# Output projections of both mixers as three passes on split operands, their residual rows through DRAM, and two narrow projections in two passes

## What is computed

```python
def gdn_mixer(x, w_in, conv_w, a_log, dt_bias, norm_w, w_out):
    p = x @ w_in                                  # [T, 6160]; its last 16 columns are b_logit and a_logit
    qkv = causal_conv_silu(p[..., :GDN_QKV], conv_w)
    ...
    o = gated_delta_rule(q, k, v, g, beta)        # chunked scan over the tokens
    o = gated_rmsnorm(o, norm_w, gate)
    return o.reshape(B, T, GDN_VAL).astype(x.dtype) @ w_out     # [T,2048] @ [2048,1024]

def gla_mixer(x, w_in, w_gk_up, b_gk, norm_w, w_out):
    p = x @ w_in                                  # its last 16 columns are gk_low
    gk_logit = (gk_low @ w_gk_up).astype(f32) + b_gk.astype(f32)
    ...
    return o.reshape(B, T, GLA_VAL).astype(x.dtype) @ w_out     # [T,1024] @ [1024,1024]

x = layer_norm(DEEP_ALPHA * x + y, ln_g[i], ln_b[i])            # behind each mixer
```

## Time and profile before

| | |
|---|---|
| time, median of 3 runs | 3444.47 us (3441.32 to 3447.07) |
| the profiled execution | 3438.09 us, of which the span of the trace is 3436.4 us |
| PE busy | 3271.8 us, 95% of the span |
| DVE, ACT, POOL busy | 1653.5 (48%), 1148.0 (33%), 479.9 (14%) us |
| chain that ended last, by engine | PE 85%, DVE 6%, ACT 4%, POOL 2% |
| L754 (GDN output products) | 512 records, 233.8 us busy, 593 ns mean |
| DMA | 168.07 MB, mean 49 GB/s |
| PE clock granted | 0.985 of full speed, mean |

### The profile page before, as it was taken

One profiled execution on the slowest core, in us unless ns is written; L12 is line 12 of the kernel. 1 busy time (PEld: TensorE's weight loads), 2 busy tenths in 40 slices (PEclk: granted clock), 3 DMA queues, 4 the chain that ended last, 5 costly groups with the idle time before them and its releaser, 6 DMA issues.

```text
span 3436.4 us, 47422 instructions
## 1 busy us (share of the span) xinstructions
PE 3271.8 (95%) x19629; PEld 2578.6 (75%) x19629; DVE 1653.5 (48%) x3418; ACT 1148.0 (33%) x2307; POOL 479.9 (14%) x745
## 2 busy tenths in 40 slices
PE   8999999999999989999989999999999999999998
PEld 6776876777587657757756688778888888888886
DVE  3443444354344454543554699576644334234334
ACT  4442343244234323413443223366632311111112
POOL 0210111021011241301352122000111000000000
PEclk9999999999999999999998999999999999999999
DMA  2210100111010101101112123100042311111111
GB/s 102 75 38 13 38 25 26 31 32 39 6 43 20 44 16 44 33 24 44 33 64 99 31 92 95 65 1 1 1 154 104 128 49 49 49 49 49 49 49 49
DMA packets 42354, 168.07 MB, mean 49 GB/s; under 512 B 5527, under 2 KB 10233, under 8 KB 36634
## 3 DMA queue, kind: packets, MB, share of 16 engines
q1 hardware_dynamic: 42138, 165.04, 14.1%
HBM read 140.91 MB, written 24.12 MB: 48 GB/s over the span
## 4 chain that ended last, share of the span: by engine, by line
PE 85%; DVE 6%; ACT 4%; POOL 2%; issue 2%; DMA 1%; SPq 0%; POOLq 0%; DVEq 0%; ACTq 0%
PE pp L584 10%; PE pp L586 10%; PE pp L585 10%; PE pp L1190 8%; PE pp L1191 8%; PE pp L1192 8%; PE pp L754 6%; PE pp L912 3%; PE pp L1163 2%; PE pp L1147 2%; PE pp L684 1%; PE pp L714 1%; PE pp L698 1%; PE pp L696 1%; PE pp L1155 1%
## 5 line engine op out<-in xcount | busy, mean ns | idle before, releaser
L584 PE MATMUL pp<-gx_hi,pw_hi 128*128 128x512 f32 x1504 | 615.1, 409 | 19.6 <-DVE pw_lo L1880 19.6
L586 PE MATMUL pp<-gx_hi,pw_lo 128*128 128x512 f32 x1504 | 592.8, 394 | 0.0
L585 PE MATMUL pp<-gx_lo,pw_hi 128*128 128x512 f32 x1504 | 592.3, 394 | 0.0
L584 PEld LDWEIGHTS pp<-gx_hi,pw_hi 128*128 128x128 f32 x1504 | 286.2, 190 | 84.8 <-DVE pw_lo L1880 20.5
L586 PEld LDWEIGHTS pp<-gx_hi,pw_lo 128*128 128x128 f32 x1504 | 285.8, 190 | 62.6
L585 PEld LDWEIGHTS pp<-gx_lo,pw_hi 128*128 128x128 f32 x1504 | 286.7, 191 | 55.0
L1190 PE MATMUL pp<-mix_hi,wt_hi 128*128 128x512 f32 x704 | 274.1, 389 | 2.8 <-DVE arena L2507 1.6
L1191 PE MATMUL pp<-mix_lo,wt_hi 128*128 128x512 f32 x704 | 273.9, 389 | 0.0
L1192 PE MATMUL pp<-mix_hi,wt_lo 128*128 128x512 f32 x672 | 261.4, 389 | 0.0
L754 PE MATMUL pp<-xT,arena 128*128 128x512 f32 x512 | 233.8, 593 | 6.1 <-DVE arena L2059 6.1
L2539 DVE TENSOR_TENSOR xT<-xT,pp 128x1024 f32<-128x1024 f32 x22 | 26.9, 1221 | 368.7 <-ACT xT L1857 368.7
(11 more groups left out here) (470 smaller groups left out, 6256.9 us busy)
## 6 DMA issues: line engine op xcount, KB each, us to landing
arena<-in_tiles_dram SPq DMA_DIRECT2D x73, 512.0 KB, 3.5
arena<-in_units_dram SPq DMA_DIRECT2D x33, 1024.0 KB, 4.9
xT<-in_tiles_dram SPq DMA_DIRECT2D x27, 512.0 KB, 4.1
xT<-in_w_outs_dram SPq DMA_DIRECT2D x6, 2048.0 KB, 8.5
arena<-gates_scratch SPq DMA_DIRECT2D x16, 512.0 KB, 3.3
xT<-in_wall_dram SPq DMA_DIRECT2D x3, 2048.0 KB, 9.6
gates_scratch<-arena SPq DMA_DIRECT2D x11, 512.0 KB, 5.1
arena<-in_xT_dram SPq DMA_DIRECT2D x8, 512.0 KB, 8.0
```

What stands on the lines that cost most here:

```text
L584: mm(b[:, hs], wh[:, c], X[0][:, k, hs], k == 0, False)
L585: mm(b[:, hs], wh[:, c], X[1][:, k, hs], False, False)
L586: m = mm(b[:, hs], wl[:, c], X[0][:, k, hs], False, k == 7)
```

## The change

1. **Output projection in three passes.** `out_half` serves both mixers and makes high x high, high x low, low x high. `turned_high` (ACT) and `turned_low` (DVE) split `oT` for each row; `weight_high` (ACT) and `weight_low` split `wo` in eight pieces of 512 columns for each group: in the GDN inside and behind the second `tee` (low parts on POOL), in the GLA in scan steps 0 and 1 (low parts on DVE, then POOL). `wo` comes as two transfers of 1 MB. The low part overwrites `wo`; the high part lies in `y`'s place (groups 0, 1, 2, 4) or in columns of `X` (3, 5).
2. **Order in the scan.** Both halves of row n-2 are made in step n; the GLA scan has ten steps instead of nine, and the layer norm of group 5 moves one step back.
3. **Rows through DRAM.** In groups 0, 1, 2 and 4 a row is loaded, added to and stored in a ring of three row buffers (`row_in`, `row_out`, `rows_through` on SP); groups 3 and 5 load all eight rows back (`rows_back`), and the rows are stored once between the mixers (`ysp`).
4. **Narrow tiles in two passes.** The two tiles hold the 16 weight columns twice; the second copy becomes the low part, and the product with the high and the low input gives both shares in different output rows, which the next product (`ident2`, or the doubled `w_up`) sums up.

```diff
-                wh, wl = parts(u) if u != "ba" else ba_W
+                both = u in ("ba", 48)
+                wh, wl = parts(u) if u != "ba" else (ba_W, None)
...
                     mm(b[:, hs], wh[:, c], X[0][:, k, hs], k == 0, False)
-                    mm(b[:, hs], wh[:, c], X[1][:, k, hs], False, False)
-                    m = mm(b[:, hs], wl[:, c], X[0][:, k, hs], False, k == 7)
+                    m = mm(b[:, hs], wh[:, c], X[1][:, k, hs], False, both and k == 7)
+                    if not both:
+                        m = mm(b[:, hs], wl[:, c], X[0][:, k, hs], False, k == 7)
...
+                _, hi, lo = turned(g, n)
                 for t in some:
-                    m = mm(b, oT[:, t * 128:(t + 1) * 128], wo[:, t * 1024 + hf * 512:t * 1024 + hf * 512 + 512], t == 0, t == 3)
+                    _, wh, wl = out_weights(g, t, hf)
+                    pe.wait_ge(("oTl", g, n), ("wol", g, t, hf))
+                    mm(b, hi[:, t, :], wh, t == 0, False)
+                    mm(b, hi[:, t, :], wl, False, False)
+                    m = mm(b, lo[:, t, :], wh, False, t == 3)
...
                 if n >= 2:
-                    out_half(g, n - 2, 1, (0, 1))
+                    out_half(g, n - 2, 0, (0, 1, 2))
                 if n < 8:
                     new_values(g, n)
                 if n >= 2:
-                    out_half(g, n - 2, 1, (2, 3))
+                    out_half(g, n - 2, 0, (3,))
...
-                if 1 <= n < 9:
-                    out_half(g, n - 1, 0, range(4))
+                if n >= 2:
+                    out_half(g, n - 2, 1, range(4))
...
+                    if q and l >= 3:
+                        for t, hf in some_weights[2 * l - 6:2 * l - 4]:
+                            weight_high(g, t, hf)
...
+            def turned_high(g, n):
+                raw, hi, _ = turned(g, n)
+                ac.wait_ge(("oT", g, n), ("op", g, n - 2, 1) if n >= 2 else high_free(g))
+                act(hi, raw, ACT.Copy).then_inc(*did("oTh", g, n))
...
             def scan_step2(g, n):
+                if 1 <= n < 9:
+                    turned_high(g, n - 1)
                 if n < 8:
                     head_squares(g, n, ob2, at("o", g, n), None)
+                if n < 2:
+                    for t in range(4):
+                        weight_high(g, t, n)
...
+                if 1 <= n < 9:
+                    turned_low(g, n - 1)
+                if n >= 2:
+                    add_half(g, n - 2, 0)
                 if n < 8:
                     head_scale(g, n, ob2)
+                if n == 0:
+                    for t in range(4):
+                        weight_low(g, t, 0)
...
+                if q:
+                    for t, hf in some_weights:
+                        weight_low(g, t, hf)
...
+            def row_in(g, n):
+                s_, r = streams.index(g), 8 * streams.index(g) + n
+                sp.wait_ge(("yst", streams[(r - 3) // 8], (r - 3) % 8) if r >= 3 else [("proj", "ba", 1), ("ba",)],
+                           ("yst", streams[s_ - 1], n) if s_ else None, [("ysp", i) for i in range(8)] + [("yT", 7, 1)] if g == 4 else None)
+                move(row_of(g, n), y_dram[n] if g else I["x"][n * 128:(n + 1) * 128, :], f"yi{r % 3}", "yin", g, n)
...
+            def rows_through(g, some):
+                for n in some:
+                    row_out(g, n)
+                    if n < 6:
+                        row_in(g, n + 2)
+                    elif g < 2:
+                        row_in(g + 1, n - 6)
...
                 sp.wait_ge(("proj", 12 * g + 11, 1))
-                move(wo, I["w_outs"][g], "wo", "d", "wo", g)
+                out_weights_in(g)
+                if g < 3:
+                    rows_through(g, range(7))
+                    sp.wait_ge(("pl", 12 * g + 12))
+                    tile(12 * g + 13)
+                    rows_through(g, [7])
```

More of the change, by code:

```diff
@@ L275, in program @@
         ob2, oT2 = take(512), take(512)
+        oT2_at = take.at[0] - 512
         qk2 = take(4096).rearrange("p (j t) -> p j t", j=4)
@@ L442, in gla_order @@
             interleave([tees(g), values(g)])
-            for n in range(9):
+            for n in range(10):
                 scan_step(g, n)
@@ L1337, in decay_logits @@
                 ac.wait_ge(("proj", "ba", 1))
-                act(baT, pair("proj", "ba")[0:16, :], ACT.Copy).then_inc(*did("bac"))
+                act(baT, pair("proj", "ba"), ACT.Copy).then_inc(*did("bac"))
             def rates():
@@ L1443, in act_program @@
                     ac.wait_ge(("d", "w_ba"))
-                    act(ba_W[0], ba_raw, ACT.Copy).then_inc(*did("ph", "ba"))
+                    act(ba_W, ba_raw, ACT.Copy).then_inc(*did("ph", "ba"))
                     split(3)
@@ L1553, in act_program @@
                     ac.wait_ge(("proj", 48, 1), ("one",))
-                    act(lowT[0:16, :], pair("proj", 48)[0:16, :], ACT.Copy).then_inc(*did("low"))
+                    act(lowT[0:32, :], pair("proj", 48)[0:32, :], ACT.Copy).then_inc(*did("low"))
                     split(50)
@@ L2646, in pool_program @@
             po.wait_ge(ended(4), ("pl", 48))
-            e.memset(lowT[0:32, :], 1.0).then_inc(*did("one"))
+            e.memset(lowT[0:64, :], 1.0).then_inc(*did("one"))
             e.memset(ATc, 0.0).then_inc(*did("zero"))
@@ L2670, in scan_step2 @@
             def scan_step2(g, n):
-                if g == 5 and 3 <= n < 8:
-                    layer_affine(n - 3, gla_rows, [("d", "ln1g"), ("d", "ln1b")], "lb", "yn2")
+                if g == 5 and 4 <= n < 9:
+                    layer_affine(n - 4, gla_rows, [("d", "ln1g"), ("d", "ln1b")], "lb", "yn2")
                 if n < 8:
                     head_norm(g, n)
-                if g == 5 and n >= 3:
-                    norm2(n - 3)
-                if g == 5 and n:
-                    layer_rstd(n - 1, "lb")
-                if g == 5 and n == 7:
+                if n == 1:
+                    for t in range(4):
+                        weight_low(g, t, 1)
+                if g == 5 and n >= 4:
+                    norm2(n - 4)
+                if g == 5 and n >= 2:
+                    layer_rstd(n - 2, "lb")
+                if g == 5 and n == 8:
                     split(73)
@@ L2828, in sp_program @@
             for g in range(4):
-                for i in range(12):
+                for i in range(1 if g else 0, 12):
                     u = 12 * g + i
@@ L2856, in sp_program @@
             tile(50)
+            for n in range(8):
+                sp.wait_ge(("yn", n))
+                move(y_dram[n], y[:, n, :], f"ysp{n % 4}", "ysp", n)
             for g in (4, 5):
-                for u in range(50 if g == 4 else 61, 61 if g == 4 else 72):
+                for u in range(50 if g == 4 else 62, 61 if g == 4 else 72):
                     sp.wait_ge(("pl", u))
                     tile(u + 1)
-                sp.wait_ge(("proj", 60 if g == 4 else 72, 1))
-                move(wo, I["w_outs"][g], "wo", "d", "wo", g)
+                    if u == 55:
+                        row_in(4, 0)
+                        row_in(4, 1)
+                    if u == 64:
+                        rows_back(5)
+                sp.wait_ge(("proj", 60 if g == 4 else 72, 1))
+                out_weights_in(g)
+                if g == 4:
+                    rows_through(4, range(7))
+                    sp.wait_ge(("pl", 61))
+                    tile(62)
+                    rows_through(4, [7])
             row(gla_rows[0], "ln1g", "ln_g1")
```

169 lines of the change are left out of this document (119 added, 50 removed).

## The result

The changed kernel takes 3390.62 us (median of four runs, 3382.85 to 3395.03), the kernel before beside it 3445.76: a ratio of 0.984 (95% interval 0.9819 to 0.9861), or 55 us less. Forecast were 68 less, 3376, with a range of 3359 to 3401. The profiled execution took 3392.56 us, its span is 3390.8 and its mean granted clock 0.978, against 0.985 in the profiled execution of before.

The account below looks back on a forecast made before the run. PE was taken to bound the kernel (95% of the span). The terms 46.1 + 6.1 - 1 + 2.6 + 3.6 + 1.8 + 5.7 + 3.0 = 67.9 us off the median 3444.5 gave 3376, range 3359 to 3401.

Parts of the forecast that it names:

- Products: Output projections of GDN and GLA: 384 products fall from 0.86 to 0.68 us each, gaining 46.1 and 23.0 us.
- Group 3: GDN's last group: one more subtraction on DVE's already loaded queue costs 0.69 us at most in three steps, taken as -1.
- Tile 49: Between groups 3 and 4: half of the tile's 5.16 us wait goes, +2.6 us, ends 0 and 5.2.
- Output weights, GDN: Splits of `wo` around the second `tee` cost nothing; ends 0 and 2 us a group if a copy waits for its transfer.
- (a): ACT and the load of `wo` set the second `tee`, both halves land together: gain 47, 3397 us, chance 0.17.
- Output weights, GLA: Start of the GLA scan: weight splits delay step 2 by 4.5 us, plus 2.5 us of clock; group 4 nets +5.7.
- Low clock: PE at half clock after the wait of 6.2 us at a GLA scan's start: a loss of 2.5 us.
- Group 5: Last GLA scan: its steps follow a loop of 10.2 us, not 8.5; gain 3.0 us, ends -4 and +9.
- (b): Output weights cost nothing and the last GLA group is not held by its loop: gain 83, 3361 us, chance 0.12.
- (c): In each of 384 products the passes hide no weight load: slower by some 110 us, 3555, chance 0.02.
- (d): The ring of three rows on SP's queue is too slow: 3505 us at 4 us for each of 32 rows, chance 0.02.
- (e): The split's chain binds every scan step, so the passes do not shorten it: gain 10, 3434 us, chance 0.03.

Follow-up runs that it names:

- the repeat: The changed kernel unaltered, timed again beside the kernel before: 3397.09 us, ratio 0.9857.
- short rows: Changed kernel, but most rows through DRAM in groups 0 to 2 and 4 move only 16 of 1024 columns: 3391.05 us, ratio 0.9839.

## Why the prediction was right, and where it was not

The time lies in the range of 3359 to 3401, but 3 us outside the forecast's own 3366 to 3388. The passes and the GDN's scan went as worked; of the 12 us that are missing by the average clock of the runs, about half are waits and half are clock, and most of it comes at the starts of the GLA scans and at the ends of groups 3 and 5.

**Products: right.** 0.69 us for each where 0.68 was forecast. The step fell by 1.36, forecast 1.44. The stage from group 0's `wo` to group 4's gained 55.1 us without low clock; the forecast's terms for it (46.1, 6.1, -1, 2.6 and 1.8) make 55.6. (With the second trace of each kernel the mean is 53.9.)

**Does the scan stay PE's: right.** 5.6 us of DVE and 3.7 of ACT in a step, forecast 5.5 and 3.7. With a pass less the step fell again, to 8.70.

**Group ends: right.** PE's waits for `oT` (6.1 us in eight) have no successor; what is left before the first pass of a product is

```profile
PE pp L803 <- DVE y L2151: 0.7, 2, 0.3
PE pp L803 <- DVE y L2149: 0.7, 2, 0.3
```

**Group 3: its sign was wrong.** The last steps take 11.61 us (from 13.29), a gain of 1.68 each, more than elsewhere: nothing was lost to DVE. **Tile 49: wrong.** The wait of 5.16 did not halve but grew:

```profile
1218.88 1.24 ACT L1458 ACTIVATE y<-y,small 128x1024 f32<-128x1024 f32 x1 [6.93 <-POOL small L2726]
...
1220.02 1.04 ACT L1338 ACTIVATE pw_hi<-arena 128x1024 fp32r<-128x1024 f32 x1
1221.10 1.22 DVE L1951 TENSOR_TENSOR pw_lo<-arena,pw_hi 128x1024 fp32r<-128x1024 f32 x1 [3.28 <-ACT pw_hi L1338]
...
1222.37 0.80 PE L630 MATMUL pp<-gx_hi,pw_hi 128*128 128x512 f32 x1 [6.25 <-DVE pw_lo L1951]
```

Read backwards, the tile's split stands behind the scale of row 7 on ACT, and that behind the last products; how close row 6 lies to row 7 is nothing to this chain. The step "row 6 now ends closer to row 7, so part of the wait goes" looked at the wrong row. Ahead of it PE waits 2.6 us for a turning that had waited 0.4, and 0.9 for a sum that had taken 2.8; with the 1.1 more here the hand-over lost some 1.4 us and did not gain 2.6. That the stage came out within 2 us all the same is in part luck: group 3 gained where a loss of 1 was forecast, and what made good the rest was not traced.

**Output weights, GDN: right.** The first high part starts at 228.64, 10 us behind the issue, forecast 226.0, and no copy waits for a transfer. From the issue to the second row's copy on ACT the four groups take 28.05, 27.33, 27.89 and 27.87 us, before 27.18, 27.78, 27.89 and 28.39: nothing in the mean. The first part of rival (a) falls. The halves landed in the order of issue, not together; but the first took 5.9 where 5.2 was forecast.

**Output weights, GLA: the mechanism was right, its size was not.** Forecast: step 2 at 12.4 us behind the issue of `wo`, a wait of 6.2, 2.5 us lost to the clock. Measured: 1426.76 - 1411.4 = 15.4 behind it, a wait of 8.98, and 10 us at half level. Of the 3.0 us, 0.7 are the landing and 2.0 the lock: POOL's first subtraction starts at 1424.02, DVE's `head_scale` at 1424.09, and each of the two stretches to 1.31. The prediction's own sign of a wrong forecast, a start over 9 us, was missed by 0.02. The prediction had the lock, but looked for it in group 5 (where it is too, below) and only for DVE operations with two SBUF inputs. The Trainium skill's page SBUF — State Buffer, section "SBUF: two separate sides", names the other case as well: a DVE operation in a two-port mode against any GpSimd operation, for the whole instruction. The trace agrees, with 2.62 us for two beside POOL and 0.61 alone; which mode `head_scale` ran in no row shows.

**Low clock: the term that was mis-sized.** It had 2.5 us for each GLA start, taken from one row of 3.5 us, and none elsewhere. The timed runs show 0.981 before and 0.974 to 0.981 after: (1 - clock) x span is 65 us before and 76 in the mean after, 11 more where the sum had 5. With 67 us gained without it, 67 less 11 is 56; the measured difference is 55, and 49 in the repeat. Worked by stage from the traces, the stages of the two starts and of group 5's end hold 13 of the 24 us more between the profiled executions; the others are in stages in which the same kernel's low clock differs by 3 to 7 from trace to trace. The rest of what is missing are waits: without clock the sum is 72.9, and the four stages up to `mx_hi` gained 2.6, 53.9, 6.8 and 4.1 (means of two traces of each kernel) where its terms without clock are 3.6, 55.6, 8.2 and 5.5.

**Group 5: the loop nearly right, its start and its end not.** The pitch is 10.6, forecast 10.2:

```profile
1731.00 0.61 DVE L2121 TENSOR_SCALAR arena<-arena,small 128x256 f32<-128x256 f32 x2 [2.79 <-POOL small L2660]
...
1741.61 0.62 DVE L2121 TENSOR_SCALAR arena<-arena,small 128x256 f32<-128x256 f32 x2 [2.77 <-POOL small L2660]
```

The lock that the prediction priced here at 0.69 us a step is in the trace: DVE's `turned_low` (L2138), 0.68 us alone, takes 1.84 beside POOL's first operation on a row, and POOL's second takes 2.72 where the first takes 2.40.

```profile
1714.05 2.40 POOL L2730 TENSOR_TENSOR y<-y,arena 128x1024 f32<-128x1024 f32 x1
...
1715.16 1.84 DVE L2138 TENSOR_TENSOR ot_lo<-arena,gx_hi 128x512 fp32r<-128x512 f32 x1
...
1716.54 2.72 POOL L2732 TENSOR_TENSOR y<-y,arena 128x1024 f32<-128x1024 f32 x1
```

So it puts some 0.3 us a step on POOL, not 0.69. From the issue of `wo` to the last `head_scale` it is 77.1 us, before 80.2. But from there to `mx_hi` it is 48.3 us, before 39.8. Two whole rows of products stand behind it (16 x 0.69 = 11.0 us), where it was one and the end of another (6.9 and 2.5), PE waits 3.29 us for the turning of row 4 that stands ahead of the last ones, and 6.07 for the next tile, where it was 3.42, and this all at a mean clock of 0.74:

```profile
1742.00:1773.00 31.00, 21.26 (x76) 16.82 (x77) 21.87 (x47) 17.72 (x38) 17.15 (x25) 0.74 0.18 61
...
1754.46 1.97 PE L971 MATMUL pp<-consts,arena 128*128 128x128 f32 x8 [3.29 <-ACT arena L1603]
...
1769.79 0.76 PE L630 MATMUL pp<-gx_hi,pe_hi 128*128 128x512 f32 x1 [6.07 <-DVE gx_lo L2311]
```

The last product was forecast 93.6 us behind the issue of `wo`; it came at 1763.7 - 1664.6 = 99.1. Of these 5.5 us, 3.0 are the start with the two steps of 8.5 behind it (turning of row 3, at the head of step 4, at 1699.44, 34.9 behind the issue instead of 31.9), 2.1 the four steps of the loop (42.9 instead of 40.8), and 0.4 the last two, for which the sum had 20.9, so not "short" ones. Behind the last product, up to `mx_hi`, it takes 26.2 us where it took 23.4, and for this the prediction had no term. So a gain of 3.0 became a loss of 5.3.

**Narrow tiles: right** for the first (3.63 us). **Rows through DRAM: right,** nothing.

**Rivals.** (a) came nearest in its number (3397) and not in its mechanism: of its 20.6 us, the second `tee` cost nothing, and the starts and group 5 lost through the lock and the clock. As its 3397 also set the upper end of the range, the range holds the time by the number of a rival whose mechanism did not occur, which is luck. (b), (c), (d) and (e) are out by the rows above: starts that cost much, passes of 0.23, short rows without gain, and a step that fell as PE's work fell. By its own figures (c)'s price at the listed duration is 1.15 x 103 = 118 us and not 110; nothing hangs on it.

Open: whether low clock in the GDN stage grows from before to after at all, and why it does with a pass less, where no longer wait of PE was found for it; and what closes group 5's loop at 10.6 to 11.3 us in every order that was tried (POOL's waits for DVE's statistics and for ACT's pass over the row each did in turn).

## What to carry to other kernels

A cheaper instruction on the bounding engine is priced well by start-to-start times; what is lost is lost where that engine stops at the seams of stages, and the waits of 3.45 to 8.98 us at the starts measured here each cost themselves and a stretch at the lower clock behind them. So put a preparation that a stage does not need for several microseconds (here the weights' splits) behind the short chain that it does need (here the second row's factor), on each of the queues. Before moving an operation of POOL, look which DVE operations it will run beside.

## What the runs showed of the hardware

- A wait of PE at the start of a GLA scan and the granted clock over the 20 us around it: 8.98 us, 0.74; 6.77 us, 0.83; 4.23 us (GLA's products as before), 0.91; 3.45 us, 0.91. That is 10, 7, 3.5 and 3.5 us at the lower level. Before, with waits of at most 2.0 us there, it was 1.00.
- DVE's scaling of 2 x 256 columns from SBUF to SBUF takes 0.61 us alone, 2.62 beside POOL's subtractions of 512 columns (1.26 each) and 4.53 beside its row operations of 1024 columns (2.4 each): each instruction is held for about one of POOL's. DVE's subtraction of 512 columns with two inputs in SBUF takes 0.68 alone and 1.84 beside POOL's row operation, and POOL's next one takes 2.72 instead of 2.40.
- The time of one kernel spreads with its low clock: two traces of the changed kernel differ by 5.9 us in span and by 5.2 us in low clock.
